# The first keys, queries and maxima of a grouped-query attention, loaded and made beside the end of the projection before it

## The reference

```
def gqa_mixer(q, k, v, z, q_norm, k_norm, cos, sin):      # 6 query heads, 2 key/value heads, 64 wide
    qh = apply_rope(head_rms(to_heads(q, 6), q_norm), cos, sin) * HEAD_DIM ** -0.5
    kh = apply_rope(head_rms(to_heads(k, 2), k_norm), cos, sin)
    vh = to_heads(v, 2)
    def attend(qblk):
        s = jnp.einsum('bkgqd,bksd->bkgqs', qblk, kh)
        p = jax.nn.softmax(s, axis=-1)
        return jnp.einsum('bkgqs,bksd->bkgqd', p, vh)
    ...
    return from_heads(o) * jax.nn.silu(z)
```

## Time and profile before

| | |
|---|---|
| median of 3 runs | 3988.6 us (3982.93 to 3988.61) |
| the profiled execution, its own time | 3988.15 us |
| its span, from the first to the last instruction | 3986.4 us |
| its mean granted TensorE clock | 0.967 |
| instructions | 56832 |
| HBM read and written | 277.65 MB, 136.32 MB |

### The profile page before, as it was taken

How to read it: one execution, slowest core, us unless ns; L and a number is a source line. 1 busy time by engine, 2 the same in 40 slices (tenths; PEclk the granted TensorE clock), 3 DMA queues, 4 the chain that set the end, 5 groups by cost and what they waited for, 6 DMA issues and landing times. The chain is left out here.

```text
span 3986.4 us, 56832 instructions
## 1 busy us (share of the span) xinstructions
PE 3727.1 (93%) x20128; PEld 3346.3 (84%) x20128; DVE 2275.3 (57%) x4273; ACT 2037.2 (51%) x4141; POOL 1237.6 (31%) x966
## 2 busy tenths in 40 slices
PE   8999999998999997969989999999989999978698
PEld 8999999998777776857789999999977777768577
DVE  5233335511788885867652333455117888859675
ACT  5233334621787776346452333346217888763464
POOL 0000011000677776435400000110006777764354
PEclk9999999999999998989989999999989999989899
DMA  4644344323211112746444443443231111126464
GB/s 156 174 125 146 120 151 159 97 70 87 55 32 37 31 34 52 186 136 186 139 152 126 131 141 118 155 162 92 64 97 43 38 32 33 31 62 182 131 190 138
DMA packets 462523, 427.15 MB, mean 107 GB/s; under 512 B 94912, under 2 KB 420512, under 8 KB 459168
## 3 DMA queue, kind: packets, MB, share of 16 engines
q1 hardware_dynamic: 461952, 422.48, 35.9%
q10 hardware_dynamic: 288, 1.05, 0.1%
HBM read 277.65 MB, written 136.32 MB: 104 GB/s over the span
## 5 line engine op out<-in xcount | busy, mean ns | idle before, releaser
L1453 POOL TENSOR_TENSOR ga_plo<-ga_prob,ga_phi 128x512 fp32r<-128x512 f32 (+1 forms) x594 | 765.9, 1299 | 1017.5 <-ACT ga_prob L1418 1003.8
L625 PE MATMUL pj_acc<-h_hi,pj_whi 128*128 128x384 f32 x2976 | 1028.3, 346 | 8.5 <-ACT pj_ring L774 4.8
L625 PE MATMUL pj_acc<-h_hi,pj_wlo 128*128 128x384 f32 x2976 | 998.0, 335 | 0.0
L625 PE MATMUL pj_acc<-h_lo,pj_whi 128*128 128x384 f32 x2976 | 997.4, 335 | 0.0
L1475 DVE TENSOR_REDUCE ga_mx<-ga_ps_x 128x1 f32<-128x512 f32 (+1 forms) x792 | 532.3, 680 | 160.2 <-PE ga_ps_x L1360 147.8
L625 PEld LDWEIGHTS pj_acc<-h_hi,pj_whi 128*128 128x128 f32 x2976 | 561.6, 189 | 15.9 <-ACT pj_ring L774 5.1
L1416 ACT ACTIVATE ga_phi<-ga_ps_s 128x512 fp32r<-128x512 f32 (+1 forms) x792 | 469.1, 592 | 196.3 <-PE ga_ps_s L1377 189.0
L625 PEld LDWEIGHTS pj_acc<-h_lo,pj_whi 128*128 128x128 f32 x2976 | 561.7, 189 | 6.4
L625 PEld LDWEIGHTS pj_acc<-h_hi,pj_wlo 128*128 128x128 f32 x2976 | 560.6, 188 | 0.0
L1418 ACT ACTIVATE ga_prob<-ga_ps_s 128x512 f32<-128x512 f32 (+1 forms) x792 | 464.9, 587 | 17.8 <-DVE ga_plo L1453 16.9
L1188 POOL TENSOR_TENSOR rq_sw<-rq_sw,rq_trig 128x384 f32<-128x384 f32 x48 | 52.4, 1093 | 1245.5 <-DMA rq_sw<-pj_ring 1245.5
(11 more groups left out here) (196 smaller groups left out, 6077.0 us busy)
## 6 DMA issues: line engine op xcount, KB each, us to landing
pj_w<-in_w_in SPq DMA_DIRECT2D x62, 512.0 KB, 3.7
dl_kv<-dil_kv SPq DMA_DIRECT2D x108, 256.0 KB, 3.0
proj<-pj_ring SPq DMA_DIRECT2D x132, 192.0 KB, 2.1
fi_z<-proj SPq DMA_DIRECT2D x36, 640.0 KB
rq_trig<-in_trig SPq DMA_DIRECT2D x48, 384.0 KB, 4.2
gqk<-rq_parts SPq DMA_DIRECT2D x48, 384.0 KB, 3.5
ml_mb<-gate_M SPq DMA_DIRECT2D x72, 256.0 KB, 4.9
y<-fi_xo SPq DMA_DIRECT2D x36, 512.0 KB, 3.2
```

Of the source, the lines that this page charges most:

```text
L625: mm = pe.matmul(acc[s % 2][:, 0:CHUNK], wt[u][:, t, :], ht[:, t, tok], start=(t == 0 and i == 0), stop=(t == KT - 1 and i == 2))
L1453: vector.tensor_tensor(p_lo[r][:, 0:w], prob[f % 2][:, 0:w], p_hi[r][:, 0:w].bitcast(F32), ALU.subtract).then_inc(sem, 1)
```

## The change

The key buffers `k_both` and `k_one` of the first key head, the queries of item 0, the maxima's buffers and an identity are put in a room (`lead_buffers`) that `project` and `attend_gqa` share at the same addresses; `project`'s other buffers are moved so that the room is free late in the stage. `h_hi` and `h_lo`, the projection's input, now belong to `project`.

In `project`, at slot 164 SP issues the six loads of these buffers, ACT fills `k_one` of the first head, and DVE clears the lower rows of `q_lom`; each first waits (`past_fourth_room`) until the room's former users are done. From slot 169 to 176 PE makes two maxima products a slot and DVE reduces them; at slot 178 PE turns them into a row and ACT copies it.

In `attend_gqa`, SP's first transfer is v. Tile 0 starts without maxima before it. The maxima of item 1 begin at tile 2, two a tile up to tile 7 instead of up to tile 3. Only the first head's values are filled and split before the tiles; the second head's fills, its keys' fills and its values' parts are put behind tiles 15, 39, 63, 87 and 111 on ACT (`SECOND_AT`) and behind tile 67 on DVE.

```diff
+def lead_buffers(k, ctx, prefix):
+    keys = [sbuf(k, ctx, prefix + n, [P, TOK], F32R) for n in ("kboth0", "kone0")]
+    queries = [sbuf(k, ctx, prefix + n, [P, QC], F32R) for n in ("qhi20", "qlom0")]
+    return (*keys, *queries, pair(k, ctx, prefix + "mx", [P, 4, 4]), pair(k, ctx, prefix + "nmax", [P, 4, 2], F32R),
+            sbuf(k, ctx, prefix + "ident", [P, P], F32R))
...
+LEAD_AT = 164
+MAX_AT = LEAD_AT + 5
+NMAX0 = DEC_SEQ // P
...
+        def maxes_beside(s):
+            return [m for m in (2 * (s - MAX_AT), 2 * (s - MAX_AT) + 1) if 0 <= m < NMAX0]
...
+        def past_fourth_room(engine):
+
+            past_third_room(engine)
+            engine.wait_ge(sa, (L + 1) * NA)
+            engine.wait_ge(sv, (L + 1) * NV)
+            engine.wait_ge(g_out, (L + 1) * 8 * DMA)
+            engine.wait_ge(g_turned, (L + 1) * 2)
...
+            def load_lead():
+                past_fourth_room(sp)
+                for u in range(2):
+                    past_transfers(sp, rot_stored, NROT, 1, NROT - u)
+                for part in range(2):
+                    sp.dma_start(k_both[part * HD:(part + 1) * HD, :].bitcast(F32), k.a["gqk"][part, 3, 0:HD, :]).then_inc(kv_in, DMA)
+                hi, lo = (k.a["gqk"][part, 0, 0:HD, SEQ:SEQ + QC] for part in range(2))
+                for dst, src in ((q_hi2[0:HD, :], hi), (q_hi2[HD:P, :], hi), (q_lom[0:HD, :], lo)):
+                    sp.dma_start(dst.bitcast(F32), src).then_inc(q_in, DMA)
+                sp.dma_start(k_one[0:HD, :].bitcast(F32), k.a["gqk"][0, 3, 0:HD, :]).then_inc(kone_in, DMA)
...
+            def max_product(m):
+                if m == 0:
+                    pe.wait_ge(kv_in, (L + 1) * 2 * DMA)
+                    pe.wait_ge(q_in, (L * GQ_HEADS + 1) * 3 * DMA)
+                    past(pe, lnss_ok, NROT, NROT)
+                past(pe, max_read, NMAX, m - 1)
+                pe.matmul(ps_s[m % 2][:].rearrange("p h t -> p (h t)"), q_hi2[:, m // 4 * P:(m // 4 + 1) * P],
+                          k_both[:, SEQ + m % 4 * QC:SEQ + (m % 4 + 1) * QC], start=True, stop=True).then_inc(max_done, 1)
...
+                for m in maxes_beside(s):
+                    max_product(m)
+                if s == MAX_AT + NMAX0 // 2 + 1:
+                    max_rows()
...
+                if s == LEAD_AT:
+                    fill_keys()
+                if s == MAX_AT + NMAX0 // 2 + 1:
+                    row()
...
+        SECOND_AT = [24 * i + 15 for i in range(6)]
...
-            m = [NKT + 2 * f, NKT + 2 * f + 1] if f < LEAD else [NKT + LEAD + f]
+            if f < 2:
+                return []
+            m = [NKT + 2 * f - 4, NKT + 2 * f - 3] if f < LEAD + 4 else [NKT + LEAD + f]
...
-            load_k(0, 0, k_both, kv_in)
-            load_k(0, 1, k_both, kv_in)
-            load(0)
-            load_k(0, 0, k_one, kone_in)
             sp.dma_start(v[:].rearrange("p n g d -> p n (g d)"),
-                         k.a["tokmaj"][:, 4 * P:5 * P].rearrange("(n p) d -> p n d", p=P)).then_inc(v_in, DMA)
+                         k.a["tokmaj"][:, 4 * P:5 * P].rearrange("(n p) d -> p n d", p=P)).then_inc(kone_in, DMA)
             load(1)
...
-            for m in range(NKT):
-                max_product(m)
-            max_rows(0)
...
+            ones_in_values(0)
+            zeros_in_values(0)
             for f in range(NTILE):
                 exp_tile(f)
+                if f == 1:
+                    act.wait_ge(kone_in, (2 * L + 2) * DMA)
+                    values_high(0)
+                    past(act, fill_v, NFILLV, NFILLQ)
+                if f == SECOND_AT[0]:
+                    ones_in_values(1)
+                if f == SECOND_AT[1]:
+                    zeros_in_values(1)
+                if f == SECOND_AT[2]:
+                    values_high(1)
+                if f == SECOND_AT[3]:
+                    zeros_in_keys()
+                if f == SECOND_AT[4]:
+                    ones_in_keys()
...
-            for m in range(NKT):
-                maximum(m)
...
+            values_low(0, 5)
...
+                if f == SECOND_AT[2] + 4:
+                    values_low(1, 8)
```

More of the change, by code:

```diff
@@ L245, in project @@
     with ExitStack() as ctx:
[L246 to L254, removed]
-        with ExitStack() as room:
[L258 to L268, removed]
+        h_lo = sbuf(k, ctx, "h_lo", [P, KT, TOK], F32R)
+        with ExitStack() as room:
+            lead = lead_buffers(k, room, "pl_")
+            t_out = pair(k, room, "tt_t", [P, CHUNK // P, P])
         with ExitStack() as room:
@@ L888, in sigmoid, with fill_keys, row @@
                 nc.scalar.activation(e[v % 2][:], e[v % 2][:], ACT.Exp).then_inc(sig_ok, 1)
+            def fill_keys():
+                past_fourth_room(act)
+                nc.scalar.copy(k_one[HD:P, :].rearrange("p (n t) -> p n t", t=SIDE),
+                               zeros[HD:P, :].unsqueeze(1).to_broadcast([P - HD, TOK // SIDE, SIDE])).then_inc(ga_fill, 1)
+                past(act, ga_fill, NFILL_GA, 1)
+                nc.scalar.copy(k_one[HD:HD + 1, :], cols["one"][HD:HD + 1, :].to_broadcast([1, TOK])).then_inc(ga_fill, 1)
+            def row():
+                past(act, row_done, NITEM, 1)
+                past(act, ga_fill_v, NFILLV_GA, 4)
+                nc.scalar.copy(q_lom[HD:HD + 1, :], ps_s[0][:].rearrange("p h t -> p (h t)")[0:1, :]).then_inc(row_ok, 1)
             def copy_chunk(n):
@@ L1348, in _ @@
         def _(pe):
-            pe.wait_ge(kv_in, (L + 1) * 2 * DMA)
             def max_product(m):
@@ L1400, in _ @@
                 if f == 2:
-                    pe.wait_ge(v_in, (L + 1) * 4 * DMA)
-                    pe.wait_ge(fill_v, (L + 1) * NFILLV)
+                    past(pe, fill, NFILL, 5)
+                    past(pe, fill_v, NFILLV, NFILLQ + 1)
                 if f >= 2:
@@ L1423, in row, with ones_in_values @@
                 nc.scalar.copy(q_lom[c][HD:HD + 1, 0:w], ps_m[0:1, 0:w]).then_inc(row_ok, 1)
-            st = Steps(act, fill, L * NFILL)
+            st = Steps(act, fill, L * NFILL + 2)
             one = cols["one"]
-            for g in range(KV_HEADS):
-                st.mark(nc.scalar.copy(k_one[g][HD:P, :].rearrange("p (n t) -> p n t", t=SIDE),
+            def ones_in_values(g):
+                st.mark(nc.scalar.copy(v_hi[g][:, :, HD:P], one.unsqueeze(1).to_broadcast([P, NT, P - HD])))
@@ L1430, in _ @@
                 st.join()
-                st.mark(nc.scalar.copy(k_one[g][HD:HD + 1, :], one[HD:HD + 1, :].to_broadcast([1, TOK])))
-                st.mark(nc.scalar.copy(v_hi[g][:, :, HD:P], one.unsqueeze(1).to_broadcast([P, NT, P - HD])))
-                st.mark(nc.scalar.copy(v_lo[g][:, :, HD:P], zeros[:, :].unsqueeze(1).to_broadcast([P, NT, P - HD])))
-            act.wait_ge(v_in, (L + 1) * 4 * DMA)
-            for g in range(2):
-                st.mark(nc.scalar.copy(v_hi[g][:, :, 0:HD], v[:, :, g, :]))
```

114 lines of the change are left out of this document (87 added, 27 removed).

## The result

Over five runs each the kernel after takes 4003.6 us (3999.5 to 4008.5) against 3988.3 (3982.9 to 3988.6): a ratio of 1.004, 95% interval 1.0026 to 1.0053. It is slower by 15 us where 12 less were forecast. The profiled execution has 4004.62 us of its own and a span of 4002.8, 16.4 more than before.

What follows compares the result with a forecast made beforehand. TensorE, busy 93% of the span, was taken as the bound, so only its standstills could pay: 19.5 us gained at the attention's start less 7.6 for fills, 11.9 us, gave 3976.5 us, range 3960 to 3988.

Steps and rivals of the forecast that it cites:

- Work moved into the projection: Projection: only PE's 16 moved products and four small row products cost time, +3.9 us a layer; the rest is covered.
- The start of the attention after: Attention start: stage begins 3.19 (layer 1: 3.48) us after the last product; v lands 8.0 us later, bounds 5.6 and 13.0.
- The wait that takes its place: After tile 3: ScalarE waits some 8 us for the first half tile of `w_out`, queued behind all loads; PE too.
- b + 24.1: Forecast start of tile 6 in layer 0: 24.1 us after the new stage begins; 23.6 in layer 1.
- The sum at the start: Up to tile 6: 10.9 and 12.5 us earlier, less 0.45 for maxima and 1.5 for slow clock; together 19.5 us.
- Fills put between the tiles: Attention tiles: fills behind 15, 39, 63, 67, 87 and 111 cost PE 3.8 us a layer, 7.6 for both.
- (1): Attention start: the weights are not late, as loads come faster; 8.0 us a layer less, 3960.5 us; chance 0.20.
- (2): Attention: the start goes as forecast and the fills between tiles are free, 3969 us; chance 0.12.
- (3): Attention tiles: the fills cost their full length, 3987 us, no change; chance 0.12.
- (4): Attention tiles: fills cost more than their length through late VectorE low halves, 14.4 us a layer, 3997.7 us; chance 0.06.

Runs made afterwards that it cites:

- a_w0: The changed kernel with the loads of the first two half tiles of `w_out` issued right behind the queries of item 1: 3986.8 us, 0.9995 of the kernel before.
- fix: The changed kernel with 160 unused bytes ahead of `h_hi` and 64 behind the lead buffers: 3976.6 us, 0.9966 of the kernel before.
- b_w128: The kernel before with 128 unused bytes ahead of the projection's weights, which also moves the smaller buffers behind them: one run, 4005.1 us.

## Why the prediction was wrong

Each of its steps on the start and on the fills held in sum, and it missed a cost that it had put at nothing.

- **"Work moved into the projection"**, 3.9 us a layer: the moved products cost 4.0 between slots 169 and 178, with no wait before a product of `pl_kboth`. Right. But this step costs the stage as if only instructions had been moved. "`project`'s other buffers are moved so that the room is free" stands in the description of the change, and the prediction gave it no price at all. This is the step that failed: with the operands at new starts every product of the stage got 2.1 ns dearer, 19 us in two layers. The same step left out of the attention's sum cost 9.5 us more.
- **"The start of the attention after"**: the new stage begins 3.36 us after the last product, as said. v landed 6.8 us after its issue in place of 8.0, and its cast began at 997.70; 1.2 us early, near the lower of the bounds of 5.6 and 13.0.
- **"The wait that takes its place"**: right in kind and in size, 7.70 us for 8, PE behind it for 5.57. The rule that the prediction took from the Trainium skill ("DMA: Bandwidth & Descriptors", "Queues, rings and completion order") fits a_w0: the same transfer, issued earlier in the same queue, is there in time. The section says in what order descriptors are consumed, and adds that completion is not first in, first out; that w can't pass the loads is the prediction's own step, and the landings bear it out here. Tile 6 came at 990.90 + 22.5, for b + 24.1.
- **"The sum at the start"**: -33.7 us for -31.3 in the same marks; v's landing is 1.2 of the 1.6 us in layer 0. The slow start at tile 6 is there, with a granted clock of 0.50, 1.2 GHz, and cost 1.5 to 1.9 us, by a_w0. The prediction read its price off a stretch at 0.51 and called it the one "after 13.3 us of" standstill. Between the two PE made the maxima, already at half clock (granted 0.50 from 988.3 to 1007.2), and then stood again, in PE's timeline of the kernel before:

```profile
1007.25 0.77 PE L1374 MATMUL ga_ps_s<-ga_qhi,ga_kboth 128*128 128x512 f32 x1 [4.81 <-ACT ga_vhi L1436]
```

  The price was right all the same.
- **"Fills put between the tiles"**: 3.8 us a layer. In `fix`, free of the other effect, the 24-tile periods from the casts of `w_out` at tiles 51, 75 and 99 are 1.07, 1.70 and 0.95 us longer than before: 3.7 us for the 0.4 + 0.7 + 1.1 + 1.1 = 3.3 of the fills that lie in them. The one at 39 costs nothing (-0.08). Right in sum; in the split, the fill at 15 cost 0.1 to 0.2 for 0.45 (read tile by tile, as the further lag of its exponentials behind those of the kernel before), the one at 63 is not to be seen, VectorE's behind tile 67 cost 1.0 for 0.7, and the period with tile 87 is 0.6 over its term, 0.4 of it at tile 77, where no fill is, which stays unexplained. PE's new waits in the kernel after, behind tiles 67, 87 and 111, where the kernel before has none (a wait is counted from the end of the product before, 0.39 us after its start, so it is shorter than the delay):

```profile
1107.39 0.50 PE L1499 MATMUL ga_ps_o<-ga_plo,ga_vhi 128*128 128x512 f32 x1 [0.69 <-POOL ga_plo L1586]
...
1138.14 0.50 PE L1484 MATMUL ga_ps_s<-ga_qhi,pl_kboth 128*128 128x512 f32 x1 [0.72 <-ACT ga_prob L1529]
...
1173.72 0.50 PE L1484 MATMUL ga_ps_s<-ga_qhi,pl_kboth 128*128 128x512 f32 x1 [0.51 <-ACT ga_prob L1529]
```

- **Rivals**: (1) did not come, the weights were late; (2) and (3) bound the fills, which came in the middle; (4), the only one on the slow side, looked for the loss in the fills' collisions, and they cost what was forecast. The loss in the attention, 10.5 us more than forecast in two layers, is nearly all the pace of the products: `fix` takes 9.5 of it back (5.1 and 4.4).

The sum is closed by `fix`: same change, same order, 224 unused bytes, 3976.6 us for the 3976.5 of the forecast. That the two agree to 0.1 us is luck of the medians, as against the kernel before beside it `fix` is 14.2 us faster for the 12 forecast; that the stretches agree (-11.3 for -11.9) is not.

Still open: why the starts matter, how moving and stationary share the loss, why 64 apart costs little in products of 384 columns (0.3 to 0.4 ns) and 3.2 to 3.3 ns in the attention's of 512, and the 0.35 ns by which the equalised projection after (173.9) stays over that of before. `finish` was left alone: its moving operand (the output weights) starts at 192 and its stationary one at 0 in both kernels, and its products of 512 columns come every 233.3 ns. Whether equal starts would speed it up no run tried.

## What to carry to other kernels

When a change adds, resizes or reorders buffers, write down the start of every matmul operand modulo 256 before and after, and price the pace of the dense stretches as a term of its own: here 1% on the products of two stages, 28 us, was more than twice the whole gain aimed at. Read that pace off regular landmarks of another engine, such as an eviction every 48 products, since durations of overlapping matmuls don't show it. And when a load is moved off the head of a queue, ask which transfer the next standstill waits for and whether it can be issued ahead of those that are needed later; here that was worth 16 us, more than the 12 that were forecast for the change itself.

## What the runs showed of the hardware that was not expected

- Products of fp32r, 128 x 128 by 384 columns, follow one another at 173.5 to 173.9 ns where the starts of both moving operands and of the stationary one are equal modulo 256 bytes, at 173.8 to 173.9 in the kernel before with 64 between them, and at 175.4 to 175.9 ns with 96 (the kernel after) or 128 between them. In the attention, at 512 columns, it is 228.2 ns, and 231.4 to 231.5 with some operands 64 apart. Which value the common start has (192, 224, 64 or, in the attention, 0) makes no difference, and distances of 256 none either.
- The Trainium skill, "SBUF — State Buffer", section "Who interferes with whom", gives TensorE two read ports, one for the moving operand and one for the weight load, and calls them independent. The runs differ: b_w128 moves the weights (and the smaller buffers behind them) by 128 bytes and leaves `h` in place, and the products go from 173.5 to 175.9 ns. The measurement decides: at this pace where the weights start relative to `h` matters. Whether it is these two reads that hold each other up, no run shows.
